# Head and rounds of an RWKV block in a three-layer transformer kernel: squares summed on TensorE, eight loads at once, a gate product on two array halves, and two instructions of each round moved

## What is computed

```python
mod = silu(c) @ mod_w[0] + mod_b[0]                 # 1024 -> 6144: sh1, sc1, gt1, sh2, sc2, gt2
h  = rms_norm(x, norm_mix_g[0]) * (1 + sc1) + sh1   # needs the first 2048 of mod only
xx = token_shift(h) - h
xr, xw, xk, xv, xa, xg = (h + xx * mu[j] for j in range(6))
r, k, v = xr @ wr, xk @ wk, xv @ wv                 # 1024 x 1024 each
w_log = -softplus(-(w0 + tanh(xw @ w1) @ w2)) - 0.5 # low rank, 64
a = sigmoid(a0 + (xa @ a1) @ a2)                    # low rank, 64
g = sigmoid(xg @ g1) @ g2                           # low rank, 160 = 128 + 32
y = wkv7_scan(...)                                  # 16 heads of 64, done in 8 chunks of 64 tokens
bonus = sum(r * k * r_k, per head) * v
x = x + (1 + gt1) * ((group_norm(y) + bonus) * g) @ wo
```

## Time and profile before

| | |
|---|---|
| median of 3 runs | 3717.54 us (3713.49 to 3733.53) |
| the profiled execution | 3723.67 us, span in the trace 3721.9 us |
| TensorE busy | 3504.2 us, 94% of the span |
| VectorE, ScalarE, GpSimd busy | 1422.2, 730.7, 376.9 us |
| mean granted TensorE clock | 0.971 of full |

### The profile page before, as it was taken

How to read it: one execution, slowest core, us unless ns; L and a number is a source line. 1 busy time by engine, 2 the same in 40 slices (tenths; PEclk the granted TensorE clock), 3 DMA queues, 4 the chain that set the end, 5 groups by cost and what they waited for, 6 DMA issues and landing times.

```text
span 3721.9 us, 54427 instructions
## 1 busy us (share of the span) xinstructions
PE 3504.2 (94%) x24266; PEld 2169.1 (58%) x24266; DVE 1422.2 (38%) x2556; ACT 730.7 (20%) x1477; POOL 376.9 (10%) x294
## 2 busy tenths in 40 slices
PE   6999998999999999999998999988989999899998
PEld 2466665588884448588884566665434444434343
DVE  4444453488642025488523444552012201211011
ACT  2223232210012025111003223332012210200001
POOL 1010010232010000223000101121000001200000
PEclk8999999999999999999998999997989999999999
DMA  5321202265641220266422101100021113499996
GB/s 186 104 79 43 76 12 81 68 181 182 194 145 35 73 75 1 68 187 186 143 74 61 43 24 35 36 13 13 31 65 33 34 46 147 176 410 409 409 409 277
DMA packets 352746, 452.62 MB, mean 122 GB/s; under 512 B 17600, under 2 KB 258496, under 8 KB 352256
## 3 DMA queue, kind: packets, MB, share of 16 engines
q1 hardware_dynamic: 352512, 449.13, 35.3%
HBM read 444.87 MB, written 4.19 MB: 121 GB/s over the span
## 4 chain that ended last, share of the span: by engine, by line
PE 87%; DVE 5%; ACT 4%; DMA 2%; issue 1%; POOL 0%; SPq 0%; POOLq 0%; DVEq 0%; ACTq 0%
PE bank L79 87%; ACT A L87 2%; DVE A L76 1%; DVE A L70 1%; DMA A<-in_w_up 1%; ACT SM L87 1%; ACT H L87 1%; DMA W<-in_w_up 0%; DVE H L70 0%; ACT A L86 0%; DVE X L76 0%; DVE SM L76 0%; POOL SM L70 0%; DVE A L73 0%; DMA A<-in_x 0%
## 5 line engine op out<-in xcount | busy, mean ns | idle before, releaser
L79 PE MATMUL bank<-A 64*64 64x64 f32 (+7 forms) x13456 | 1051.4, 261 | 62.0 <-ACT A L87 42.0
L79 PEld LDWEIGHTS bank<-A 64*64 64x64 f32 (+3 forms) x13456 | 816.9, 148 | 312.2 <-issue 144.8
L79 PE MATMUL bank<-A,W 128*128 128x512 f32 (+2 forms) x2272 | 792.5, 504 | 9.5 <-DVE A L76 3.6
L79 PE MATMUL bank<-H,W 128*128 128x512 f32 (+3 forms) x1824 | 718.8, 548 | 26.9 <-ACT H L87 14.1
L79 PEld LDWEIGHTS bank<-A,W 128*128 128x128 f32 (+1 forms) x2272 | 420.6, 189 | 327.1 <-issue 287.4
L79 PEld LDWEIGHTS bank<-H,W 128*128 128x128 f32 (+2 forms) x1824 | 344.5, 193 | 365.1 <-issue 334.0
L87 ACT ACTIVATE A<-bank 128x512 f32<-128x512 f32 (+6 forms) x544 | 243.2, 450 | 1454.5 <-PE bank L79 1444.6
L70 DVE TENSOR_TENSOR A<-bank,A 128x256 f32<-128x256 f32 (+2 forms) x315 | 145.9, 475 | 402.3 <-PE bank L79 381.2
L79 PE MATMUL bank<-A,H 128*64 128x512 f32 (+1 forms) x1096 | 281.0, 595 | 11.8 <-ACT H L87 8.1
L70 POOL TENSOR_TENSOR A<-A 128x512 f32<-128x512 f32 (+1 forms) x111 | 157.3, 1423 | 1077.3 <-ACT A L87 371.9
L87 ACT ACTIVATE A<-A 128x512 f32<-128x512 f32 (+1 forms) x224 | 131.0, 610 | 447.1 <-DVE A L70 360.0
(11 more groups left out here) (165 smaller groups left out, 2392.8 us busy)
## 6 DMA issues: line engine op xcount, KB each, us to landing
W<-in_mod_w SPq DMA_DIRECT2D x48, 1024.0 KB, 7.1
A<-in_w_gate SPq DMA_DIRECT2D x47, 1024.0 KB, 18.5
A<-in_w_up SPq DMA_DIRECT2D x42, 1024.0 KB, 18.6
A<-in_w_down SPq DMA_DIRECT2D x40, 1024.0 KB, 18.7
W<-in_mlp_up SPq DMA_DIRECT2D x64, 512.0 KB, 5.5
W<-in_mlp_down SPq DMA_DIRECT2D x128, 256.0 KB, 4.0
W<-in_w_mod SPq DMA_DIRECT2D x24, 1024.0 KB, 5.2
W<-in_w_down SPq DMA_DIRECT2D x24, 1024.0 KB, 18.4
```

The costliest lines, as they stand in the source:

```text
L79: return self.e.matmul(o, l, r, start=start, stop=stop, skip_group_check=True)
```

## The change

Five edits, all in the RWKV layer's head and rounds.

1. The squares of the eight x tiles go to a buffer of their own (`SQ8`), and PE sums them with eight products of 128 x 512 against ones, each as soon as its square is there. GpSimd does nothing in the head.
2. The eight loads of mod0a are issued at once: the last three go to slots in `A` that other layers use. The order on PE becomes: wide product of group 1, its turn, row sum 0, wide product of group 3, row sum 2, turn of 3.
3. The narrow product of 32 columns is split by tokens into two of 256, which go to two column groups of the array (output rows 0 to 31 and 64 to 95 of bank 5). The low-rank products write banks 3, 4 and 5, so that banks 0, 1 and 2 are free for the first round.
4. The bonus product on DVE stands three slots later, and the last of the eight tiles of `dv_mod0` two slots later.
5. `pe_row0(r)` is issued in round r+1: behind the fetch for r = 0 and 1, and in the chain for r = 2 to 7.

```diff
+        def sp_mod0a(sp):
+            n = 0
+            for g in range(4):
+                for hf in range(2):
+                    if n == NS:
+                        ring.slots, ring.turn = NS + MORE, NS + MORE - 3
+                    load_mod(sp, "mp" if g % 2 else "md", "mod0a", a["mod_w0"], g, hf)
+                    n += 1
+            ring.slots, ring.turn = NS, 3
...
+            pe.wait_ge(s_dv, ndv["c", 1])
+            wide(1)
+            turned(1)
+            pe_mod_row(pe, "mod0a", 0, 6)
+            wide(3)
+            pe_mod_row(pe, "mod0a", 2, 6)
+            turned(3)
...
+        SQ8 = A[:, 16384:20480].rearrange("p (k t) -> p k t", k=8)
+
+        def ac_squares0(ac):
+            for k in range(KT):
+                ac.wait_ge(s_ac, nac["x", k])
+                ac.act(SQ8[:, k, :], x3[:, k, :], SQUARE).then_inc(s_ac, nac("sq", "mix0", k))
+
+        def pe_squares0(pe):
+            for k in range(KT):
+                pe.wait_ge(s_ac, nac["sq", "mix0", k])
+                m = pe.mm(BK[7][:, :], C("ones"), SQ8[:, k, :], k == 0, k == 7)
+            m.then_inc(s_pe, npe("ss", "mix0"))
...
-            outs = BK[0][:, :], BK[1][:, :], BK[2][0:32, :]
+            outs = BK[3][:, :], BK[4][:, :]
...
+                    for n, rows in enumerate(GROWS):
+                        m = pe.mm(BK[5][rows, 0:256], narrow, src[:, 256 * n:256 * n + 256], f, l)
...
-            ac.act(ZG[0:32, 512:1024], BK[2][0:32, :], ACT.Sigmoid).then_inc(s_ac, nac("lo", 3))
+            for n, rows in enumerate(GROWS):
+                ac.act(ZG[0:32, 512 + 256 * n:768 + 256 * n], BK[5][rows, 0:256], ACT.Sigmoid).then_inc(s_ac, nac("lo", 3 + n))
...
-            if ct < 3:
-                pe_row0(pe, ct)
+            if ct in (1, 2):
+                pe_row0(pe, ct - 1)
...
-            yield from idle(3)
+            yield from idle(6)
             dv.wait_ge(s_pe, npe["bon", ct])
             dv.wait_ge(s_ac, nac["v", ct])
             dv.tt(yg[:, ct, :], BK[3][:, :], V, MUL).then_inc(s_dv, ndv("bo", ct))
-            yield from idle(6)
+            yield from idle(3)
...
-                    if c == 7 and ct + 3 < 8:
-                        pe_row0(pe, ct + 3)
+                    if c == 7 and ct + 2 < 8:
+                        pe_row0(pe, ct + 2)
...
-            left = {0: (s_ac, nac["lo", 1]), 1: (s_ac, nac["lo", 2]), 2: (s_ac, nac["lo", 3]), 3: (s_ac, nac["lo", 3])}
+            turned = s_ac, nac["x", 7]
+            left = {0: turned, 1: turned, 2: turned, 3: (s_ac, nac["lo", 1])}
```

More of the change, by code:

```diff
@@ L326, in sp_mod, with dv_mod_group @@
                 yield
             yield
-        def dv_mod(dv, key, o, n, cc, bias, bc, on_pe=(), late=0):
+        def dv_mod_group(dv, key, g, cc, acc, before):
+            for hf in range(2):
+                k, there = ring["md", key, g, hf]
+                dv.wait_ge(ring.sems[k], there)
+                v = wv(k, 0, (0, P), (4, 512))
+                for j in range(4):
+                    c = cact[:, cc + 4 * hf + j:cc + 4 * hf + j + 1]
+                    if hf == 0 and j == 0:
+                        if before:
+                            dv.wait_ge(*before)
+                        m = dv.ts(acc, v[:, j, :], c, None, MUL, None)
+                    else:
+                        dv.wait_ge(s_dv, ndv.n)
+                        m = dv.stt(acc, v[:, j, :], c, acc, MUL, ADD)
+                    m.then_inc(s_dv, ndv() if j < 3 else ndv("free", "md", key, g, hf))
+                yield
@@ L330, in dv_mod, with mod_acc @@
+        def mod_acc(g):
+            return rowb[:, (g % 2) * 512:(g % 2) * 512 + 512]
+        def dv_mod(dv, key, o, n, cc, bias, bc, late=0):
             dv.wait_ge(s_dv, ndv["c", 1])
             for g in range(n // 512):
[L332 to L350, removed]
@@ L351, in dv_mod @@
+                yield from dv_mod_group(dv, key, g, cc, mod_acc(g), (s_pe, npe["row", key, g - 2]) if g >= 2 else None)
                 yield
@@ L355, in dv_mod, with pe_mod_row, pe_mod @@
             yield
-        def pe_mod(pe, key, n, cc, bc, on_pe=(), after=None, late=0):
+        def pe_mod_row(pe, key, g, bc):
+            pe.wait_ge(s_dv, ndv["free", "md", key, g, 1])
+            for j in range(4):
+                m = pe.mm(BK[bc][:, 4 * g + j:4 * g + j + 1], mod_acc(g)[:, j * 128:(j + 1) * 128], C("ones", 1), True, True)
+            m.then_inc(s_pe, npe("row", key, g))
+        def pe_mod(pe, key, n, bc, after=None, late=0):
             yield from idle(late)
@@ L361, in pe_mod @@
                 pe.wait_ge(s_dv, ndv["mod", after])
[L362 to L382, removed]
@@ new lines, in pe_mod0a, with wide, turned @@
+        def pe_mod0a(pe):
+            def wide(g):
+                for hf in range(2):
+                    k, there = ring["mp", "mod0a", g, hf]
+                    pe.wait_ge(ring.sems[k], there)
+                    v = wv(k, 0, (0, P), (4, 512))
+                    for j in range(4):
+                        m = pe.mm(BK[5][0:1, :], cact[:, 4 * hf + j:4 * hf + j + 1], v[:, j, :], hf == 0 and j == 0, hf == 1 and j == 3)
+                    m.then_inc(s_pe, npe("free", "mp", "mod0a", g, hf))
+            def turned(g):
+                pe.wait_ge(s_ac, nac["rowp", g])
+                for j in range(4):
+                    m = pe.mm(BK[6][:, 4 * g + j:4 * g + j + 1], rowp[0:1, j * 128:(j + 1) * 128], C("ones")[0:1, 0:1], True, True)
+                m.then_inc(s_pe, npe("row", "mod0a", g))
+            pe.wait_ge(s_dv, ndv["c", 1])
[5 more added lines that the diff above has]
+            turned(3)
```

122 lines of the change are left out of this document (59 added, 63 removed).

## The result

The changed kernel takes 3697.47 us (median of 9 executions, 3683.23 to 3706.06) against 3725.79 us for the kernel before on the same chips (9 executions, 3713.49 to 3733.53). The ratio is 0.9922, with a 95% interval from 0.9905 to 0.9940: 29 us less, 22 to 35 us. The same kernel timed once more later gave 0.9928 (0.9911 to 0.9945).

The account below looks back on a forecast made before the run. The prediction took TensorE, busy 94% of the span, to bound the kernel. Its terms, 7.9 + 6.3 + 1.3 + 9.0 + 7 = 31.5 us, off the median 3717.5 gave 3686 us, range 3672 to 3704.

Parts of the forecast that it names:

- Head: Start of the layer: squares on TensorE and the new order bring the bias 8.4 us earlier, 7.9 us after weight waiting.
- The 0.5 for low-rank weights: End of the head: TensorE waits for late low-rank weights, at worst 1.0 us, 0.5 us taken off the saving.
- The sentence on the loads: Head: without eight loads at once, the last would start only when a slot is free and TensorE would miss it.
- Narrow product: Low-rank part: two token halves overlap on column groups, saving 6.3 us, from 0 to 6.9 us.
- the rule on weight loads: Trainium skill: loads overlap running products only across row groups; 64 narrow loads would lie bare, gain about nothing, not 6.3 us.
- Banks: Behind the low-rank part: the fetch of round 0 waits for no bank, saving 1.3 us.
- Waits in the rounds: Ends of rounds 2 to 7: shorter TensorE stalls save 2.1 us in round 2 and five times 1.38, together 9.0 us.
- Clock: Rounds: fewer low-clock spells begin behind shorter waits, saving 7 us, from 0 to about 14.
- the clock spells stay: Rival, chance 0.15: low-clock spells in the rounds remain, as the row sums' surroundings are nearly unchanged; saving 24.5 us, 3693 us.
- a new wait: Rival, chance 0.10: in the rounds TensorE stalls as long on state, copy or next mask; 9.0 and 7 gone, 3702 us.
- the halves overlap: Rival, chance 0.06, claimed the opposite: in the low-rank part the second half starts only after the first; 3692 us.
- the head did gain: Rival, chance 0.03, claimed the opposite: no gain there, since weights or VectorE's group 2 end last; 3694 us.

Follow-up runs that it names:

- four groups at once: Changed kernel with the narrow product split by tokens over four column groups, all eight narrow products of a part behind its wide ones; ratio 0.9906.
- before, with the rounds' edits: Kernel before with only row sums a round later and bonus product and eighth tile later; ratio 0.9974.
- the row sums in their own round: Changed kernel with each row sum issued in its own round again, bonus product and eighth tile as changed; ratio 0.9973.
- the bonus product early: Changed kernel with the bonus product back ahead of the seventh tile and the state on VectorE; ratio 0.9949.
- all further steps: Changed kernel with narrow and head one-row products on four column groups, a separate accumulator for group 2, seventh tile behind the state; ratio 0.9873, median 3679.07 us.

## Why the prediction was right, point by point

The forecast was 31.5 us less, to 3692 us from the profiled execution or 3686 from the median shown; measured were 29 (22 to 35) and 27 (20 to 33) us. The direction, the mechanisms and the places were right; the terms were off in both directions, and that their sum is so near is in part luck: three terms came out 3 us larger in the first profile, and the totals leave 3 to 7 us less for the clock than its 7. In absolute time the kernel came out 11 us above 3686, and 8 of them are the start: the median of three executions of the kernel before was 3717.54 us, that of nine 3725.79.

**Head, 7.9 us forecast.** It was 10.0 in the first profile and 7.1 in the second (57.71 - 50.62). 1.7 of the 2.1 us that the first has over the forecast is the clock spell ahead of the squares, which came in three of six profiles. The 0.5 for low-rank weights was not spent: the wait at 47.71 is one for ScalarE's h and as long as before (2.21 us). The sentence on the loads was the one wrong step here, and cost nothing because it had no term in the sum.

**Narrow product, 6.3 us.** Measured 6.9 (3.4 with xx and 3.5 with h), which was the upper bound. The ends of the overlap cost less than I had allowed (and 16 times 0.42 is 6.7, not the 6.8 that the prediction has). The trace's row decided against the rule on weight loads, and four groups at once confirmed the row.

**Banks, 1.3 us.** The 1.34 us are gone in every kernel that has the edit, and there in the one kernel of the experiments that lacks it (before, with the rounds' edits).

**Waits in the rounds, 9.0 us.** Measured 9.5: five times 1.35 (0.41 left; the prediction says 0.37, and its own rows give 260.39 - 260.05 = 0.34), and the whole 2.84 of round 2 instead of 2.1. I had forgotten that the row sum, once it needs nothing, is itself work to fill the wait behind it.

**Clock, 7 us.** Its mechanism shows in the traces at the size forecast, but the totals give less. First the place that the term was meant for, from the row sum of round 2 to some 10 us behind the last one. Windows of the kernel before, of the row sums in their own round and of the bonus product early, all with waits of 1.00 us or more:

```profile
203.00:534.00 331.00, 313.26 (x4837) 215.49 (x4838) 155.69 (x281) 98.01 (x227) 36.54 (x27) 0.95 0.17 54
186.00:518.00 332.00, 313.51 (x4838) 215.51 (x4838) 154.77 (x281) 98.16 (x228) 36.55 (x27) 0.95 0.17 54
185.00:555.00 370.00, 353.72 (x5805) 247.11 (x5802) 182.02 (x333) 114.40 (x268) 42.89 (x32) 0.96 0.16 51
```

And of the changed kernel in its two profiles and of the kernel before with the rounds' edits, whose waits are 0.41 us:

```profile
183.00:540.00 357.00, 343.43 (x5754) 239.00 (x5754) 181.58 (x332) 113.97 (x265) 42.97 (x32) 0.99 0.16 53
185.00:547.00 362.00, 348.63 (x5774) 244.07 (x5772) 182.36 (x332) 114.07 (x266) 42.90 (x32) 0.97 0.16 52
201.00:561.00 360.00, 346.83 (x5780) 241.95 (x5777) 184.12 (x332) 114.08 (x266) 42.92 (x32) 0.98 0.17 52
```

Added up over windows of 1 us, the low clock lasted 30.6 us in each of the first three profiles, and 10.2, 20.4 and 17.0 us in the others; over all nine profiles with waits of 0.41 us the mean is 16.6. That is 14 us less at half the clock, or 7 us of time. The clock fell close to the row sum (from 0.4 us ahead of its start to 3.4 us behind it) at all 17 waits of 1.00 us or more, and at 23 of the 45 waits of 0.41 us. So the long waits do bring spells of low clock. The two experiments that bring waits back agree in size: 9.4 + 7 = 16 us for the row sums in their own round, against 17 to 19 measured, and 3.3 + 7 = 10 for the bonus product, against 8 to 10.

The totals of the change itself don't show these 7 us. The four other terms add up to 27.7 us with the head of the first profile (10.0 + 6.9 + 1.3 + 9.5) and to 24.8 with that of the second, and the two timings gave 29 and 27, so about 0 to 4 us are left for the clock. The rounds' edits alone gained 9.7 us for 9.5 us of waits. What stands against the 7 us is low clock farther on: between there and 25 us past the start of the layer's output product it lasted 17.1 us in the kernel before and in the first profile of the changed kernel, but 34.1 in its second, 41.0 with the rounds' edits alone, 30.7 to 37.5 in eight of the other experiments and 20.5 in the one with all further steps. Over whole executions the mean granted clock was 0.969 before (46 executions) and 0.971 and 0.970 changed (9 and 6); the difference is worth 6 us, and the head's 17 us at half clock account for about as much. Whether the change brings the later low clock, or the one profile of the kernel before had less of it than most, no run here shows: the kernel before was profiled once. The uncertainty of each total, 5 to 9 us, is as large as the term. Of the rival "the clock spells stay" (24.5 us) and the forecast (31.5 us) neither is nearer to the 27 and 29 us measured.

Of the other rivals, a new wait of more than 0.41 us did not appear at the ends of the rounds, the halves overlap, and the head did gain.

## What to carry to other kernels

Ask for each wait of the bounding engine what ends it, and then which of the two engines' orders can be changed: here the reader was moved to where it needs nothing (some 6 us), and an instruction without a reader in sight was moved behind one that is waited for (some 3 us). Work that the bounding engine does in a stretch where it would stand still is free: eight products instead of two on TensorE saved 8 to 10 us, for they took the place of GpSimd's chain of 9.9 us. A product with few output columns should be split by its moving side over column groups; putting it next to others of the same form was run only together with the four groups. A wait also costs what the clock does behind it: count the low clock in the same stretch of every profile, and of the stretches behind it too. And compare stages between profiles at the same granted clock, since two profiles of one kernel differed by 19 us.

## What the runs showed of the hardware that I had not expected

Products of 32 output columns on four column groups overlap almost fully, with their weight loads: 64 instructions of 128 moving columns in 1.90 us, 0.030 us each (a quarter of the 0.107 us that such an instruction would take at the pace of 0.43 us for 512 columns is 0.027), and the same with a single output column (64 in 1.93 us). Split so, a one-row product of 1024 x 512 takes 1.93 us instead of 7.03.

The same program has its spells of low clock at different places in different executions: the squares took 7.13 us in one profile and 8.78 in another behind nearly the same idle time (3.12 and 2.88 us), and the rounds ran at a mean of 0.98 and 0.95.

In the rounds the clock fell at every one of 17 waits of 1.00 us or more ahead of a row sum, and at 23 of 45 waits of 0.41 us.
